# Two attention stages: the last V block cut by token tile, the V copy one pair later, and another order of the scalar engine's work in the late head pairs

## What is computed

```
q, k, v = split(x @ w_qkv)                  # 16 heads of 64 channels
q, k    = rope(q), rope(k)                  # first attention: causal
q, k    = rmsnorm(q), rmsnorm(k)            # second one: neighborhood bias, no causal mask
s       = q @ k.T (+ causal mask, or + bias)
p       = softmax(s)
out     = (p @ v) @ w_out
```

## Time and profile before

| | value |
|---|---|
| median of three timed runs | 2016.65 us (2015.17 to 2016.82) |
| the profiled execution: time, and the span of its instructions | 2015.27 us, 2013.5 us |
| PE, DVE, ACT busy | 98%, 63%, 44% of the span |
| granted TensorE clock over the span | 0.997 |
| first attention, from its last V block to its end | about 484 to 549 us |
| second attention, from its last V block to its end | about 1094 to 1168 us |

### The profile page before, as it was taken

One profiled execution on the slowest core, in us unless ns is written; L12 is line 12 of the kernel. 1 busy time (PEld: TensorE's weight loads), 2 busy tenths in 40 slices (PEclk: granted clock), 3 DMA queues, 4 the chain that ended last, 5 costly groups with the idle time before them and its releaser, 6 DMA issues.

```text
span 2013.5 us, 32415 instructions
## 1 busy us (share of the span) xinstructions
PE 1964.8 (98%) x12722; PEld 1609.4 (80%) x12722; DVE 1264.3 (63%) x1623; ACT 890.5 (44%) x1282; POOL 165.1 (8%) x198
## 2 busy tenths in 40 slices
PE   7999999999999999999999999999999999999999
PEld 6689788887688879888878678877767888898887
DVE  7874854576764556755757655577986554576543
ACT  4452354434543434444545544434434444435442
POOL 2242100000010010000012011002100000000000
PEclk9999999999999999999999999999999999999999
DMA  8411355644266636655455157553224556455544
GB/s 300 123 53 57 126 208 195 204 173 157 101 213 211 194 129 209 201 187 190 158 194 173 68 170 235 190 196 126 104 74 150 195 180 216 147 181 186 189 163 149
DMA packets 93046, 336.03 MB, mean 167 GB/s; under 512 B 11230, under 2 KB 11364, under 8 KB 92623
## 3 DMA queue, kind: packets, MB, share of 16 engines
q1 hardware_dynamic: 85824, 311.62, 45.3%
q0 software_dynamic: 7120, 22.95, 4.1%
HBM read 332.43 MB, written 1.05 MB: 166 GB/s over the span
## 4 chain that ended last, share of the span: by engine, by line
PE 88%; DVE 8%; ACT 1%; issue 1%; POOL 1%; DMA 0%; SPq 0%; DVEq 0%; POOLq 0%; ACTq 0%
PE acc L391 42%; PE acc L495 21%; PE acc L464 9%; DVE w_lo L1680 2%; PE acc L978 1%; PE aux L895 1%; DVE w_lo_extra L1680 1%; PE aux L934 1%; PE aux L679 1%; POOL rstd L2564 1%; PE aux L966 1%; PE acc L666 1%; PE aux L955 1%; DVE operand_lo L1701 1%; PE aux L514 0%
## 5 line engine op out<-in xcount | busy, mean ns | idle before, releaser
L1680 DVE TENSOR_TENSOR w_lo<-w_raw,w_hi 128x1024 fp32r<-128x1024 f32 x376 | 450.8, 1223 | 179.7 <-ACT w_hi L1239 174.6
L1239 ACT ACTIVATE w_hi<-w_raw 128x1024 fp32r<-128x1024 f32 x376 | 388.1, 1057 | 302.9 <-PE acc L391 111.9
L391 PE MATMUL acc<-w_hi,operand_hi 128*128 128x512 f32 x848 | 338.4, 399 | 14.6 <-DVE operand_lo L1887 12.1
L391 PE MATMUL acc<-w_hi,operand_lo 128*128 128x512 f32 x848 | 332.0, 392 | 0.0
L391 PE MATMUL acc<-w_lo,operand_hi 128*128 128x512 f32 x848 | 331.6, 391 | 0.0
L1680 DVE TENSOR_TENSOR w_lo_extra<-w_raw,w_hi_extra 128x1024 fp32r<-128x1024 f32 x212 | 251.5, 1221 | 51.0 <-ACT w_hi_extra L1239 46.6
L1239 ACT ACTIVATE w_hi_extra<-w_raw 128x1024 fp32r<-128x1024 f32 x212 | 216.0, 1058 | 83.2 <-DMA w_raw<-in_weights 69.2
L2110 DVE TENSOR_TENSOR hidden_ff<-silu_ff,acc 128x256 f32<-128x256 f32 x132 | 49.5, 417 | 251.1 <-ACT silu_ff L1457 251.1
L391 PEld LDWEIGHTS acc<-w_hi,operand_hi 128*128 128x128 f32 x848 | 159.8, 188 | 49.9 <-DVE operand_lo L1887 11.9
L391 PE MATMUL acc<-w_hi_extra,operand_hi 128*128 128x512 f32 x496 | 196.1, 395 | 1.1 <-DVE w_lo_extra L1680 0.8
L391 PE MATMUL acc<-w_hi_extra,operand_lo 128*128 128x512 f32 x496 | 193.5, 390 | 0.0
(11 more groups left out here) (516 smaller groups left out, 3231.8 us busy)
## 6 DMA issues: line engine op xcount, KB each, us to landing
w_raw<-in_weights SPq DMA_DIRECT2D x588, 512.0 KB, 4.6
ln_gain<-in_gains POOLq DMA_DIRECT2D x7, 512.0 KB, 4.7
bias_at<-in_rpb POOLq DMA_DIRECT2D x12, 256.0 KB, 6.2
ln_gain<-in_ln_g POOLq DMA_DIRECT2D x4, 512.0 KB, 5.0
ln_bias<-in_ln_b POOLq DMA_DIRECT2D x4, 512.0 KB, 6.3
vec_rw<-in_vec POOLq DMA_DIRECT2D x3, 512.0 KB, 4.7
l_rw<-in_lora SPq DMA_DIRECT2D x1, 1152.0 KB, 10.5
iclr_rw<-in_xT SPq DMA_DIRECT2D x2, 512.0 KB, 4.5
```

Of the source, the lines that this page charges most:

```text
L391: mm = pe.matmul(acc[:, 2 * pair + t, :], (ah, al)[x][:, kt, t * P:(t + 1) * P], weight(w, q + i)[:, kk * 512:(kk + 1) * 512], start=(kt = ...
L1239: act.activation(weight(0, q), raw[:, s, :], ACT.Copy).then_inc(w_hi[s], 1)
L1680: dve.tensor_tensor(weight(1, q), raw[:, s, :], weight(0, q).bitcast(F32), ALU.subtract).then_inc(w_lo[s], 1)
```

## The change

In PE's list `last_block` takes the token tiles to be done. Quarter 2's tile 1 moves behind `turn_probs(0)`. Quarter 3's tile 0 moves behind `values(0)`, and its tile 1 into round 1, behind `turn_probs(1)`. The wait for the V copy moves from round 1 to round 2. In the last round the wait for the exponentials is dropped (the scaled probabilities are waited for in `turn_probs` in any case). On DVE the V copy moves from round 0 to round 1. `ahead(q + 23, 1)` moves to round 1 in the second attention and stays in round 0 in the first one. In ACT's late pairs both exponentials come before `output_hi`.

```diff
-            def last_block(i):
+            def last_block(i, tiles=(0, 1)):
                 s = (q + 20 + i) % SLOTS
-                pe.wait_ge(w_lo[s], nth(q + 20 + i))
-                for t in range(TT):
+                if 0 in tiles:
+                    pe.wait_ge(w_lo[s], nth(q + 20 + i))
+                for t in tiles:
                     mm = part_tokens(q + 20, i, 1, t)
-                mm.then_inc(w_used[s], 1)
+                if 1 in tiles:
+                    mm.then_inc(w_used[s], 1)
...
             last_block(1)
-            last_block(2)
+            last_block(2, (0,))
             pe.wait_ge(m["probs_ready"], due(m["probs_ready"], TT))
             scores(1)
             turn_probs(0)
-            last_block(3)
+            last_block(2, (1,))
             pe.wait_ge(m["in_done"], due(m["in_done"]))
             values(0)
+            last_block(3, (0,))
             held = 4 if near else 3
             for p in range(1, PAIRS):
-                pe.wait_ge(m["probs_ready"], due(m["probs_ready"], TT))
+                probs = due(m["probs_ready"], TT)
                 if p + 1 < PAIRS:
+                    pe.wait_ge(m["probs_ready"], probs)
                     scores(p + 1)
...
                 if p == 1:
-                    pe.wait_ge(m["in_done"], due(m["in_done"]))
+                    last_block(3, (1,))
                 elif early:
+                    if p == 2:
+                        pe.wait_ge(m["in_done"], due(m["in_done"]))
                     project_part(p - 2, 1)
...
                 if p + 1 < PAIRS:
                     exponentials(p + 1, 0)
-                if p >= late:
-                    output_hi(p)
-                else:
+                if p < late:
                     copy_probs()
                 if p + 1 < PAIRS:
                     exponentials(p + 1, 1)
-                if p == 0:
+                if p == (1 if near else 0):
                     ahead(q + 23, 1)
-                if p < late:
-                    output_hi(p)
+                output_hi(p)
...
-                if p == 0:
+                if p == 1:
                     used(q + 23)
                     dve.tensor_copy(VTOK[:, :, 512:1024], acc[:, 2:4, :]).then_inc(m["in_done"], 1)
+                if p == (1 if near else 0):
                     ahead(q + 23, 1)
```

## The result

| | before | changed |
|---|---|---|
| median of the timed runs (13 each) | 2016.33 us | 2021.01 us |
| ratio, 95% interval | | 1.0025 (1.0018 to 1.0032) |
| the profiled execution: time, span | 2015.27, 2013.5 us | 2018.64, 2016.6 us |
| granted TensorE clock over the span | 0.997 | 0.993 |

The kernel became slower by a quarter of a percent. The forecast was 2019.0 us with a range of 2015.8 to 2022.0, and the likeliest case was "within 0.2%". The time lies in the range and on the forecast's side. One execution of the experiment with the split moved in both attentions took 3280.63 us at a granted clock of 0.557 and is left out of its ratio.

A forecast was written before the change was run, and what follows sets the result against it. PE, busy 98% of the span, was taken as the bound, so only its waits could move. Terms 0.0 - 2.6 - 1.4 + 5.2 + 1.7 = +2.9 us gave 2018.2 or 2019.6 us; forecast 2019.0, range 2015.8 to 2022.0.

The forecast's parts named there:

- the likeliest case: Whole run: time within 0.2% (4.0 us) of the kernel before, counted as the same; chance 0.68.
- Each named wait: First attention: ahead of pair 0's turn, values(0), pair 1's low part; second: ahead of pair 0's turn and values(0).
- The late waits: PE's 1.39 us waits for exponentials, last two rounds of first attention, last of second; removal gains 2.6 and 1.4 us.
- The net of the first start: First attention, first rounds: new waits and two cut quarters cancel the removed waits; 0.0 us, give or take 0.6.
- The start of the second attention without the clock: Second attention, first rounds: new waits and cut quarters less the removed wait make it 5.2 us slower (4.2 to 6).
- The step that decides: Second attention: ACT's split of q+26 waits for all of quarter 2, delaying pair 0's copy; PE idles 5.4 us before values(0).
- The clock: Second attention: after the 5.4 us wait PE's clock falls to 0.57 for 4 us, costing 1.7 us (0 to 3.4).
- Rival 2: Clock falls in first attention too, or two slow stretches in second: another 1.7 us, +4.6 us, 2020.7 us; chance 0.2.
- The sum for the stages: Both attentions, starts, late pairs and clock together: 2.9 us slower.
- a fall in the first attention: First attention: low clock around the new 0.9 and 1.2 us waits, another 1.7 us; part of Rival 2, chance 0.2.
- late waits that stay: Late pairs: another operand ends last, gains shrink to 1.4 of 4.0 us; +5.5 us, 2021.7 us; chance 0.08.
- The base: Whole run: starting time for the sum; profiled execution 2015.27 us gives 2018.2, the median 1.4 us higher gives 2019.6.

## Why the prediction was right, and where it was off

**What PE would wait for.** Each named wait came: forecast 0.9, 1.2 and 0.4 us in the first attention, measured 0.82, 1.06 and 0.24; in the second 0.4 and 5.4, measured 0.3 and 5.2. The late waits went as written (0.2 us left of the first). The net of the first start, 0.0 forecast, was +0.1. The late gains, 2.6 and 1.4 forecast, were 2.6 and 1.5. The start of the second attention without the clock, 5.2 forecast, was 5.0 (33.7 - 28.7).

**The step that decides.** It was the split of q+26. Its own row said that ACT waits for quarter 2, and the start list of ACT and DVE said what is queued behind. The experiment that moved only the split showed it.

**The clock.** The term was undersized: 1.7 us forecast from one stretch, 2.3 measured. The wait of 5.2 us brought a low stretch twice as long as one of 2.9 us does (1108.4 to 1115.2), 1.8 us of it inside the wait. The forecast had laid the whole low stretch behind the wait, 4 us at 0.57; it was 5.0 us at 0.50. Rival 2 named two slow stretches in the second attention, at a price of 3.4 us: that is nearer to what came, and the part inside the wait makes it 2.3. Both ends of the range (0 and 3.4) held it.

**What lay outside.** The sum for the stages was +2.9, measured +3.3. The timed runs gave +4.7 and, repeated, +4.0 (medians). The remaining 0.7 to 1.4 us are in no term of the forecast, which took all other stages as unchanged. The clock of the runs (0.9933 to 0.9935 against some 0.996) shows that they weren't. With them the first measurement went to 0.25%, on the side "slower by over 0.2%", to which I had given 0.28; the repeated one, at 0.17%, fell into the likeliest case. The sum stood close to the border, and which side a measurement gave is luck; the steps of the rivals that I had put there (a fall in the first attention, late waits that stay) didn't come in the changed kernel. A fall behind a late wait of 1.39 us did come in two experiments, though, and so the earlier trace rows with its one quiet window was too little to call such a wait safe. The changed kernel no longer has such a wait.

**The base.** I put the forecast between the profiled execution and the median. The profiled execution of the kernel before lost 6.4 us to low clock by its windows, that of the changed kernel 11.4, so that neither an unchanged stage nor the base can be taken as fixed to better than a few us.

## What to carry to other kernels

Before moving a group of matmuls as a filler, list who waits for its release and what stands behind that waiter in the other engines' queues; a prefetch that waits for a buffer belongs behind the work that the bound engine needs next. If every order of the fillers gives the same time, the fillers aren't the bound: list what the other engines do up to the point where PE needs their result, both their work and their own waits, and look for a prefetch that stands ahead of a maximum or a copy. And compare stretches of a stage between profiles before reading a ratio of 0.1 or 0.2%.

## What the runs showed of the hardware

A wait of PE of one and the same length is followed by a low clock in one kernel's execution and not in another's: 1.39 us (a low stretch behind it in two of the four kernels that kept both such waits in the first attention), 1.88 us at line 879 (in six of the fourteen profiled executions). Each single low stretch cost some 1.7 us of PE work (0.57 to 0.60 over 4 us), the one behind 5.2 us of waiting 2.3 to 2.5. Six calls of the filler in that wait kept the clock at 1.00. An edit that removes 4 us of waits in one stage can lose a part of them in a later one without touching it, by a stretch of this kind.
